# A two-layer hybrid encoder on one core: a new step order, half a weight chunk more ahead, joined further passes of the experts, and products nobody reads

## The reference

```python
h = rms_norm(x, attn_norm_w[l]);  proj = h @ w_in[l]
y_a = windowed_gqa_sink(...)   # 6 heads, 2 key heads, window 128, sink, ALiBi
y_b = ssd_mixer(...)           # 6 heads, convolution, scan forward and backward, gate, rms_norm
y_c = diff_attention(...)      # 4 heads, each the difference of two softmaxes, rms_norm
x = x + concat([y_a, y_b, y_c]) @ w_out[l]
h = rms_norm(x, ffn_norm_w[l])
x = x + hierarchical_moe(h, ...)   # 1 of 4 groups, then 2 of its 8 experts per token
```

## Time and profile before

| | us |
|---|---|
| median of 3 runs | 1186.97 |
| profiled execution | 1185.0 |
| its span, first to last instruction | 1183.3 |
| TensorE busy with products | 923.9 |
| VectorE busy | 354.0 |
| ScalarE busy | 202.8 |
| DMA queue of SP, share of 16 engines | 88.0% |

### The profile page before, as it was taken

How to read it: one execution, slowest core, us unless ns; L and a number is a source line. 1 busy time by engine, 2 the same in 40 slices (tenths; PEclk the granted TensorE clock), 3 DMA queues, 4 the chain that set the end, 5 groups by cost and what they waited for, 6 DMA issues and landing times.

```text
span 1183.3 us, 26463 instructions
## 1 busy us (share of the span) xinstructions
PE 923.9 (78%) x11004; PEld 587.3 (50%) x11004; DVE 354.0 (30%) x1165; ACT 202.8 (17%) x600; POOL 8.1 (1%) x24
## 2 busy tenths in 40 slices
PE   7999889667678786986699988996666666765954
PEld 6877745333344443553388777453333333433532
DVE  4666343111112232231166645321111111111213
ACT  2275211000001010110124652110000000000001
POOL 2000000000000000000000000000000000000000
PEclk9999989887889998998899999898888888888977
DMA  9853489999999999999996326899999999999995
GB/s 340 319 223 143 151 337 428 429 429 430 429 428 428 429 429 428 412 427 431 405 399 257 124 99 252 353 429 428 430 431 427 431 430 428 431 429 428 428 427 208
DMA packets 50633, 436.17 MB, mean 369 GB/s; under 512 B 9408, under 2 KB 13760, under 8 KB 24640
## 3 DMA queue, kind: packets, MB, share of 16 engines
q1 hardware_dynamic: 50496, 434.26, 88.0%
HBM read 433.20 MB, written 1.05 MB: 367 GB/s over the span
## 4 chain that ended last, share of the span: by engine, by line
PE 46%; DMA 39%; DVE 4%; issue 4%; SPq 2%; DVEq 2%; ACT 1%; ACTq 0%
DMA ring<-in_w_up 38%; PE ps L623 13%; PE ps L711 8%; PE ps L639 5%; PE ps L855 5%; PE ps L648 3%; PE ps L591 3%; PE ps L727 2%; PE ps L611 2%; SPq L462 1%; PE ps L716 1%; DMA ring<-in_w_in 1%; SPq L464 1%; PE ps L824 1%; PE ps L774 1%
## 5 line engine op out<-in xcount | busy, mean ns | idle before, releaser
L623 PE MATMUL ps<-ring,xg 128*32 128x256 f32 x4352 | 314.2, 452 | 173.9 <-DMA ring<-in_w_up 168.6
L623 PEld LDWEIGHTS ps<-ring,xg 128*32 128x32 f32 x4352 | 170.0, 129 | 301.4 <-issue 239.9
L1204 DVE SCALAR_TENSOR_TENSOR th<-th,ps 128x128 f32<-128x128 f32 x72 | 20.7, 287 | 588.1 <-ACT th L977 588.1
L639 PE MATMUL ps<-ring,actT 128*32 128x256 f32 x2304 | 139.2, 382 | 14.1 <-issue 13.2
L977 ACT ACTIVATE th<-ps 128x128 f32<-128x128 f32 x72 | 20.0, 277 | 510.2 <-PE ps L623 474.2
L639 PEld LDWEIGHTS ps<-ring,actT 128*32 128x32 f32 x2304 | 69.0, 109 | 75.3 <-DVE actT L1208 22.6
L591 PE MATMUL ps<-xh,Pb 128*32 128x256 f32 x1152 | 79.5, 394 | 23.4 <-issue 19.4
L711 PE MATMUL ps<-hT,ring 128*128 128x256 f32 x416 | 93.5, 382 | 1.0 <-ACT hT L1014 0.8
L711 PEld LDWEIGHTS ps<-hT,ring 128*128 128x128 f32 x416 | 77.8, 190 | 15.0 <-issue 4.4
L648 PE MATMUL ps<-ysb,PwT 32*128 32x256 f32 x992 | 71.6, 403 | 0.0
L981 ACT ACTIVATE ysb<-ps 128x256 f32<-128x256 f32 x64 | 24.5, 383 | 223.9 <-PE ps L639 223.9
(11 more groups left out here) (259 smaller groups left out, 681.5 us busy)
## 6 DMA issues: line engine op xcount, KB each, us to landing
ring<-in_w_down SPq DMA_DIRECT2D x62, 2048.0 KB, 40.4
ring<-in_w_gate SPq DMA_DIRECT2D x60, 2048.0 KB, 45.2
ring<-in_w_up SPq DMA_DIRECT2D x60, 2048.0 KB, 46.9
ring<-in_w_in SPq DMA_DIRECT2D x6, 2048.0 KB, 15.5
ring<-in_w_out SPq DMA_DIRECT2D x4, 2048.0 KB, 18.6
ring<-in_w_gate SPq DMA_DIRECT2D x8, 1024.0 KB, 29.3
ring<-in_w_up SPq DMA_DIRECT2D x8, 1024.0 KB, 31.3
ring<-in_w_in SPq DMA_DIRECT2D x6, 1024.0 KB, 16.0
```

The source lines that it names most:

```text
L623: last = mm(b_gate[j * SLOTS:(j + 1) * SLOTS, 0:2 * GQ], tokens[:, k, :], ring[:, low:high + 1:high - low, o:o + GQ], start=(k == 0), stop ...
L639: last = mm(b_y[j * SLOTS:(j + 1) * SLOTS, 0:DQ], actT[:, c * SLOTS:(c + 1) * SLOTS], ring[:, slot, o:o + DQ], start=(c == 0), stop=(c == ...
```

## The change

- `ORDER` is a new order of the mixer's steps. `outA` is cut into `outA` (chunks 0 to 2, the first head group) and `outC` (chunks 3 to 5, the scan's); `outC.0` waits for `yn` and the second piece of `w_out`.
- The squares of the three chunks are added on VectorE (`ya.1`, `ya.2`), and `sS` sums one chunk instead of three.
- Each `fT.j` waits for its own `xc2.j` only, and the router's product is cut into four steps `lk`. `fT.0` and `fT.1` stand between the products of `outB`. ScalarE scales only `fT.3`.
- `busy.0` makes 5 products between `seed` and `cnt`; 2 more stand between the first gather and the wait for `ov`. Nobody reads them.
- The tables and the router matrix move into memory of the mixer. Over them, once `ov` is done, `spare` takes the first half of down of expert 3 (`SPARE_E`); only the second half then waits for a slot. GpSimd makes the tables again for layer 1 after expert 3 of layer 0, and `wr` is loaded by itself behind `w_out`.
- For experts 2 to 30 the last further pass and the expert's own pass are joined in `pe_extra_n`: combine of the expert before, the two `hidden` one after the other, and the rest interleaved; the block ends in a branch to the next expert. A further pass keeps its hidden sums in the bank of the places.
- The four small steps of the gates (`route` on VectorE) stand behind the first `tokens_ready`.

The core of the diff (the functions below keep their other lines):

```diff
+SPLIT = PLACE["front", 0] + RING + LATE
+SPARE_E = WEIGHTS[SPLIT][1]
+assert WEIGHTS[SPLIT][0] == "down"
...
 ORDER = """
-    sq xT.0 xT.1 xT.2 xT.3 rs par xbc.0 xbc.3 conv.0 xbc.2 silu.0 conv.3 xbc.1 aq.0 dc.1 conv.2 conv.1 lam xbc.4 silu.1
-    silu.2 conv.4 dc.0 dt silu.3 dta silu.4 ak aq.2 cum cB sc.0 aS.0 sc.1 cumT nm.0 cb.0 z.0 zs.0 seg.0.0 seg.0.1
-    row.0.1 v rows.0 aq.1 row.0.0 seg.1.0 seg.1.1 xs.0 pT.0 row.1.0 xs.1 row.1.1 sc.2 sc.3 seg.2.0 nm.1 aS.1 ck.0 nm.2
-    y.0 cb.1 rows.1 row.2.0 nm.3 yq.0 z.2 seg.3.0 seg.2.1 row.2.1 aS.2 seg.3.1 row.3.0 row.3.1 pT.1 sc.4 seg.4.0 zs.2
-    nm.4 z.1 seg.4.1 seg.5.0 zs.1 rows.2 y.1 seg.5.1 yq.1 ck.1 row.4.0 row.4.1 row.5.1 cq.0 row.5.0 pT.2 oa.0 sc.5 cq.1
-    y.2 pT.3 cS.0 nm.5 yq.2 pT.4 oa.1 sc.6 sc.7 sS cS.1 pT.5 nm.6 yn oa.2 pT.6 sc.8 sc.9 nm.7 sc.10 outA.0 pT.7 outA.1
-    sc.11 nm.8 sc.12 pT.8 sc.13 nm.9 od.0 outA.2 pT.9 oS.0 od.1 oS.1 outA.3 cn outB.0 outB.1 outB.2 outB.3 xc2.0 xc2.1
-    xc2.2 sa.0 sa.1 xc2.3 sa.2 fT.0 sd fT.1 fT.2 fT.3 rs2 lg seed wt cnt xn2 rank ov route
+    sq xT.0 xT.1 xT.2 xT.3 rs par xbc.1 xbc.3 conv.1 conv.3 xbc.0 dc.1 conv.0 silu.0 xbc.4 xbc.2 conv.2 conv.4 silu.1
+    silu.2 aq.2 dc.0 dt silu.3 dta ak aq.0 lam xs.0 cum silu.4 sc.0 sc.1 cumT nm.0 aS.0 cB z.0 cb.0 nm.1 pT.0 rows.0
+    aq.1 seg.0.0 zs.0 seg.0.1 seg.1.0 seg.1.1 row.0.0 v row.0.1 row.1.1 xs.1 row.1.0 aS.1 sc.2 rows.1 sc.3 nm.2 cb.1
+    ck.0 nm.3 y.0 seg.2.0 z.2 row.2.0 seg.2.1 seg.3.0 yq.0 pT.1 row.2.1 seg.3.1 aS.2 row.3.0 row.3.1 sc.4 seg.4.0 z.1
+    rows.2 nm.4 zs.1 seg.4.1 y.1 yq.1 ck.1 zs.2 ya.1 seg.5.0 row.4.1 row.4.0 seg.5.1 cq.0 pT.2 row.5.1 sc.5 oa.0 row.5.0
+    nm.5 pT.3 cq.1 yq.2 y.2 cS.0 oa.1 pT.4 sc.6 ya.2 sc.7 sS cS.1 pT.5 sc.8 nm.6 yn oa.2 sc.9 sc.10 pT.6 nm.7 outA.0
+    outC.0 pT.7 sc.11 outA.1 nm.8 outC.1 sc.12 sc.13 pT.8 nm.9 outA.2 od.0 pT.9 outC.2 od.1 oS.0 oS.1 outA.3 cn outC.3
+    outB.0 outB.1 xc2.0 sa.0 xc2.1 fT.0 outB.2 sa.1 xc2.2 fT.1 outB.3 xc2.3 fT.2 lk.0 lk.1 sa.2 fT.3 sd lk.2 lk.3 rs2 lg
+    seed busy.0 wt cnt xn2 rank ov route
...
+FT_ON_ACT = (3,)
...
-LATE_FREED_BY = [("y", S_H // 2 - 1), ("outB", NQ - 1), ("lg",)]
+LATE_FREED_BY = [("y", S_H // 2 - 1), ("outB", NQ - 1), ("lk", NQ - 1)]
...
+BUSY = (5, 2)
+FIRST_OUT = min(PE_STEPS.index(("outA", 0)), PE_STEPS.index(("outC", 0)))
...
+        wr = sb("wr", [P, KC, NG + NE], at=m)
+        upto = sb("upto", [P, P], at=m)
+        since = sb("since", [P, P], at=m)
+        before = sb("before", [P, P], at=m)
+        ones = sb("ones", [P, P], at=m)
+        dist = sb("dist", [P, TT * P + P], at=m)
+        distw = sb("distw", [P, TT * P + P], at=m)
...
+        m2[0] = -(-m2[0] // 512) * 512
+        spare = sb("spare", [P, CHUNK // 2], at=m2)
...
+                    if n == SPARE_E:
+                        to, src = to[:, FC // 2 * D:], src[:, FC // 2 * D:]
...
-                    elif step[0] == "lg":
+                    elif step[0] == "lk":
                         sp_.wait_ge(done["dve"], nth(li, "dve", ("rs2",)))
...
+            def load_wr(li):
+                sp_.dma_start(wr[:, :, :], w_router[li, :, :].rearrange("(k p) n -> p k n", p=P)).then_inc(wr_ready, 16)
...
+                    if i == SPLIT:
+                        sp_.wait_ge(done["pe"], nth(li, "pe", ("ov",)))
+                        sp_.dma_start(spare[:, :], w_down[li, SPARE_E, :, :].rearrange("(p c) d -> p (c d)", c=FC)[:, 0:FC // 2 * D]
+                                      ).then_inc(spare_landed, 16)
...
+                        load_wr(0)
+                    if li > 0 and i == PIECES - 1:
+                        sp_.wait_ge(M["down_mm"], (li - 1) * NE + SPARE_E + 1)
+                        load_wr(li)
...
+            for li in range(DEPTH):
+                if li > 0:
+                    pool.wait_ge(M["down_mm"], (li - 1) * NE + SPARE_E + 1)
+                for t in (upto, since, before, ones):
...
+                to = b_places[:, 0:2 * GQ] if S is V else b_gate[:, 0:2 * GQ]
...
+                elif e == SPARE_E:
+                    pe.wait_ge(spare_landed, 16 * (li + 1))
...
+                    if e == SPARE_E and e < NE - 1 and c == FC // 2:
+                        pe.wait_ge(signal, count)
+                    w = spare if e == SPARE_E and c < FC // 2 else ring[:, slot, :]
...
-                        pe.wait_ge(done["act"], nth(li, "act", *(("yq", c) for c in range(S_IN // P))))
-                        for t in range(TT):
-                            for c in range(S_IN // P):
-                                last = mm(bank[:, t:t + 1], zT[:, c, t * P:(t + 1) * P], ones[:, 0:1],
-                                          start=(c == 0), stop=(c == S_IN // P - 1))
+                        pe.wait_ge(done["dve"], nth(li, "dve", ("ya", S_IN // P - 1)))
+                        for t in range(TT):
...
-                            w_half = [piece(len(W_IN_PIECES)), piece(len(W_IN_PIECES) + 1)]
+                            w_half = [piece(len(W_IN_PIECES)), None]
                             pe.wait_ge(done["act"], nth(li, "act", ("oa", 0), ("oa", 1), ("oa", 2)))
+                        elif s == ("outC", 0):
+                            w_half[1] = piece(len(W_IN_PIECES) + 1)
                             pe.wait_ge(done["dve"], nth(li, "dve", ("yn",)))
                         elif s == ("outB", 0):
                             pe.wait_ge(done["dve"], nth(li, "dve", ("cn",)))
                         for t in range(TT):
-                            for c in range(2 * REP) if kind == "outA" else range(2 * REP, MC):
+                            for c in range(*{"outA": (0, REP), "outC": (REP, 2 * REP), "outB": (2 * REP, MC)}[kind]):
...
-                        if s[1] == 0:
-                            pe.wait_ge(done["dve"], nth(li, "dve", ("xc2", NQ - 1)))
+                        pe.wait_ge(done["dve"], nth(li, "dve", ("xc2", s[1])))
...
-                    elif kind == "lg":
-                        pe.wait_ge(router_ready, (li + 1) * 16 * NROUTER)
+                    elif kind == "lk":
+                        pe.wait_ge(wr_ready, (li + 1) * 16)
                         n = NG + NE
-                        for k in range(KC):
-                            if k % 2 == 0:
-                                by = reader(("fT", k // 2))
-                                pe.wait_ge(done[by], nth(li, by, ("fT", k // 2)))
+                        bank = ps[BANK[("lg",)]]
+                        by = reader(("fT", s[1]))
+                        pe.wait_ge(done[by], nth(li, by, ("fT", s[1])))
+                        for k in (2 * s[1], 2 * s[1] + 1):
...
+                    elif kind == "busy":
+
+                        for j in range(BUSY[s[1]]):
+                            last = mm(ps[BANK["fT", 2]][:, j % 2 * SEQ:(j % 2 + 1) * SEQ], ident[:, :], x[:, j % 2, 0:SEQ], start=True, stop=True)
...
+                for j in range(BUSY[1]):
+                    mm(b_gate[:, 0:SEQ], ident[:, :], x[:, j % 2, 0:SEQ], start=True, stop=True)
...
-                    left_at[n] = nc.cur_bb
-                    nc.switch_bb(f"pe_expert_{n}")
+                    left_at[n] = nc.cur_bb if e < 3 else left_at[n - 1]
+                    nc.switch_bb(f"pe_expert_{n}", parent=left_at[n])
...
+                    own = 2 <= e < NE - 1
+                    if own:
+                        pe.wait_ge(M["y_copied"], n - 1)
+                        pe.wait_ge(M["places_copied"], n - 1)
+                        combine(M, PwT[(e - 1) % 2], ysb)
+                    def whole(count):
+                        with pe.Fori(0, count) as j:
+                            i = prev + j + 1
+                            pe.wait_ge(V["prep_ready"], 2 * i)
+                            gather(V, Pb[(e + 1) % 2])
+                            if n > 1:
+                                pe.wait_ge(M["places_copied"], n - 1 if e == 0 else n)
+                            places(V, Pw[(e + 1) % 2])
+                            pe.wait_ge(V["places_copied"], i)
+                            pe.wait_ge(V["xg_ready"], i)
+                            hidden(V, xg[(e + 1) % 2], li, e)
+                            if n > 1:
+                                pe.wait_ge(M["y_copied"], n - 1)
+                            pe.wait_ge(V["actT_ready"], i)
+                            down(V, li, e)
+                            pe.wait_ge(V["y_copied"], i)
+                            combine(V, PwTx, ysbx)
+
+                    if own:
+                        with pe.If(more_e > 1):
+                            whole(more_e - 1)
+                    else:
+                        whole(more_e)
+                    if not own:
+                        pe.br(f"pe_expert_{n}")
+                        continue
+
+                    i = prev + more_e
+                    pe.wait_ge(V["prep_ready"], 2 * i)
+                    gather(V, Pb[(e + 1) % 2])
+                    pe.wait_ge(M["places_copied"], n)
+                    places(V, Pw[(e + 1) % 2])
```

(34 more changed lines are left out.)

143 lines of the change are left out of this document (58 added, 85 removed).

## The result

The changed kernel takes 1199.40 us (1198.57 to 1205.05, 4 runs) against 1186.59 us for the kernel before (1184.99 to 1187.02): a ratio of 1.0121, interval 1.0088 to 1.0153. It is slower by 1.2%, where the prediction had 1178.0. Its profiled span is 1196.8 us against 1183.3.

The account below looks back on a forecast made before the run. The weight stream at 429 GB/s plus its stops was taken to bound the kernel. Gains of 1.6 (layer 0), 1.2 (middle) and 6.2 us (layer 1), together 9.0, took 1186.97 to 1178.0 us; range 1169.5 to 1184.

Parts of the forecast that it names:

- What bounds the kernel: Whole kernel: time is the weight stream's bytes at 429 GB/s plus its stops, before both layers' experts and amid layer 0's.
- Joined passes: Layer 0's experts: joining hides 2.9 us of waits six times, 17 us, ending a 1.19 us stop: 1.2 us gained.
- Rival C: Further passes: cold branches into longer blocks add 6.2 us waits for code; 1205.2 with seven, chance 0.07.
- Order and sums of squares: Both mixers: fewer square-sum products bring outB.0 1.0 us earlier per layer; additions and changed waits count as zero.
- rival A: Both mixers: the new order also closes TensorE's waits, up to 3.2 us more per layer, 1171.6; chance 0.13.
- Choice and layer 0: Before the experts: routing's choice 1.1 us earlier; in layer 0 SP reaches the spare load 1.6 us earlier.
- Fillers: Before the first experts: unread products may delay the counts 0.3 us; holding the clock, layer 1's first expert takes 3.6 us.
- rival D: First experts: the unread products don't hold the clock, front 1.3 us later, 0.5 us lost, 1178.5; chance 0.68 including the forecast.
- Half a chunk: Before layer 1's experts: 1 MB loaded ahead gives 2.4 us of stream, so the whole 4.5 us stop goes.
- Clock in the mixer: Layer 1's last outA: outC.2 breaks up the small products, so 7.11 us becomes 5.4, a gain of 1.7 us.
- Moved loads and constants: Mixer and gates: moved router loads, remade tables and later gate steps count as nothing, the gates perhaps 0.4 us won.

Follow-up runs that it names:

- the kernel with the loop moved away: Changed kernel with the loop for second and later further passes put behind all other blocks, so joined blocks run straight through: 1186.8 us, ratio 0.9997.
- the padded kernel: The unjoined kernel plus 132 never-run products behind the loop of each further pass, spacing blocks as far apart as joined ones: 1207.18 us, ratio 1.0168.
- the old order: The unjoined kernel with the steps up to the third heads' group norm ordered as in the kernel before: 1183.36 us, ratio 0.9971.
- the unjoined kernel: The changed kernel with one line altered, so no expert joins its further pass to its own: 1176.93 us, ratio 0.9919 against the kernel before.
- the kernel with the parameters later: The unjoined kernel with layer 1's parameter and router loads nine chunks later in SP's order: 1178.11 us, ratio 0.9934.

## Why the prediction was wrong, point by point

**What bounds the kernel** held. In the kernels that differ only in the further passes the time moved, within 1 us, by what the stream lost.

**The step that failed is "Joined passes":** "17 us against a stop of 1.19, so the stop goes: 1.2 us". It set the saving against a stop and put the waits for code that the joining adds at nothing. The stop grew to 28.7 us. The saving of 2.9 us per pass was right, as the kernel with the loop moved away shows (16.6 us a block). What was left out are 40.2 us of further waits: 16.6 us for the jump over a loop that isn't run, 2.1 to 5.1 us in each of five blocks, 16.4 us inside the experts behind a return, and 7.2 us for a third entry and longer ones.

Rival C had the mechanism and gave 1205.2 with seven waits, 5.8 us above the measured 1199.40; it had a chance of 0.07. Its counter-argument was one row, 0.82 us at 398.81, the entry of a neighbouring further pass. As far as it goes it held: where one joined block follows another, the entry shows no wait. But that row has nothing that is jumped over, and it was taken to speak for the inside of the block and for the returns too. Nor does it hold at every distance, as the padded kernel shows. C's own formula does fairly with the measured waits: 1.2 + 40.2 - 17.4 = 24.0 us against 28.7. That C's 27.2 us came so near is in part luck: the waits weren't seven of 6.2 us but ten more, mostly of 2 to 5 us.

**Order and sums of squares.** Zero for the waits was too low. From the norm's sums to outB.0 it takes 33.5 us instead of 36.25, so the idle time of 4.17 us has shrunk to some 2 (0.61 for `ptb`, 0.56 for `st`, 0.74 for `pbuf`, 0.22 for `yc`). That is 2.7 us per layer where I had 1.0, so of the 3.2 us that rival A adds about half came. The 1.0 us for the sums of squares can't be seen by itself: in the old order, with four products and VectorE's additions, layer 1 takes 126.6 us to outB.0; before it took 127.1, of which 1.7 is the clock. That is 1.2 us more where 1.0 less was forecast. So the additions, put at nothing, or another part of the change in that kernel, took back more than the products gave; which of them isn't shown.

**Choice and layer 0.** The choice came 3.5 us earlier instead of 1.1, and 4.55 instead of 1.6 at SP's first load behind the parameters. Of the last, 1.5 us comes from the issue of `fnk`, 5.13 us instead of 6.62.

**Fillers.** They hold the first expert at full clock, as said, and are worth 2 to 4 us, where rival D had put their lack at 0.5. "0.3 us late" for the counts was too low in layer 0: 1.5 us, because the seed took 5.07 instead of 3.70 us.

**Half a chunk.** Right: the stop of layer 1 is gone, and returns as 3.2 us without it.

**Clock in the mixer.** The 1.7 us came as forecast, but by luck: the reason given was that outC.2 breaks up the small products, and it comes with the old order too. What made the clock fall in the kernel before stays open.

**Moved loads and constants** cost nothing that a run shows; no run took them out alone. Without the joined term, 1.2 us, the forecast would have been 1179.2, and the unjoined kernel takes 1176.93.

## What to carry to other kernels

Before code of an engine is made longer or given a loop that is usually skipped, count what is jumped over: a row that shows a branch to be cheap holds for its distance only. A saving of 3 us of TensorE per pass is worth nothing if its slack is already enough (the stop was 1.2 us), while each wait for code of 2 to 7 us draws on the same slack. And small strided loads are to be issued where the queue has nothing else to issue: between chunks they block it, for 26 us here, and moving them from one such place to another gains nothing.

## What the runs showed of the hardware

- A jump over 66 products that are not run costs TensorE 2.1 to 5.4 us of "issue", an entry into a block far from the code just run 6.2 to 8.0 us, once 10.95, and behind a return a further 2.0 to 5.3 us in the middle of straight code. In the changed kernel the products go on 3.8 us after the start of a 16 KB transfer of code at an entry, and 2.3 to 2.5 us after it elsewhere. The queue of instruction transfers has 96 packets before, 97 in the unjoined kernel, 110 in the changed one.
- Behind the long ones of such waits TensorE's clock is at 0.50: products right behind an entry take 2.09 us instead of 1.15.
- In layer 0 the clock fell to 0.50 at 143 us, while TensorE had no idle time above 0.20 us: it was between transposes and products of 36 columns, and the seed behind them took 5.07 us. In layer 1 the same steps left it at full (748.13: 3.70 us) in the changed kernel, but not in the one without fillers (5.39). What decides is open.
- Eight loads of 0.5 KB with a stride take SP 5.1 us to issue at 151 us of the unjoined kernel, with 5 us of chunks still to come, and 22.3 us at 180 us of the kernel with the parameters later, with over 20 us of chunks still to come. The 1704 packets of 4 bytes of all the small loads then take 1.0 us of each of the 16 engines.
